# A hybrid diffusion step with expert retrieval: the latent phase entered before the prompt's routing, its products spread over the front, late chunks routed by pairs of heads

## The reference

```python
h = rmsnorm(x) * (1 + sc_a) + sh_a
q, k, v, xr, xg, ga, gr = split(h @ w_in)
attn = windowed attention(q, k, v)        # latent queries also read cached keys
rnn  = rglru(dwconv(xr))                  # forward and backward scan over the tokens
a_out = attn @ w_attn_o
r_out = (rnn * gelu(xg)) @ w_rnn_o
x = x + g_a * ((sigmoid(ga) * a_out + sigmoid(gr) * r_out) @ w_out)
h = rmsnorm(x) * (1 + sc_f) + sh_f
# experts, chunk by chunk of 128 tokens: 1 chunk of the prompt, 4 of the latent tokens
s = (h @ w_q) against 2 x 128 sub-keys for each of 8 heads
st, it = top_k(s, 16)                     # per head and side
best, pos = top_k(st[0][:, None] + st[1][None, :], 16)   # 16 experts of 16384 per head
e = it[0] * 128 + it[1] at pos
act = gelu(u_tab[e] . h)                  # 128 rows of 4 KB per token
x = x + g_f * sum(softmax(best) * act * v_tab[e])        # 128 more rows of 4 KB per token
y = rmsnorm(x)
```

## Time and profile before

| | us |
|---|---|
| median of 3 runs | 2618.7 |
| their range | 2607.69 to 2623.31 |
| the profiled execution | 2609.64 |
| its span in the trace | 2607.8 |
| DVE busy | 1808.8 (69%) |
| PE busy | 1918.0 (74%) |
| POOL busy | 1026.9 (39%) |
| ACT busy | 475.3 (18%) |
| DMA moved | 753.44 MB, mean 289 GB/s |

### The profile page before, as it was taken

One profiled execution on the slowest core, in us unless ns is written; L12 is line 12 of the kernel. 1 busy time (PEld: TensorE's weight loads), 2 busy tenths in 40 slices (PEclk: granted clock), 3 DMA queues, 4 the chain that ended last, 5 costly groups with the idle time before them and its releaser, 6 DMA issues.

```text
span 2607.8 us, 20641 instructions
## 1 busy us (share of the span) xinstructions
PE 1918.0 (74%) x6333; PEld 1129.0 (43%) x6333; DVE 1808.8 (69%) x3658; ACT 475.3 (18%) x1195; POOL 1026.9 (39%) x1028
## 2 busy tenths in 40 slices
PE   6789676989978999993666776469999999000085
PEld 2568552444437548441222333256666666000032
DVE  1341386987777115499888999788877566999955
ACT  0451201533004200111112342180000000000011
POOL 0000001324640000125776776634434445777574
PEclk9889787999989999997998998989999999555599
DMA  8656554657970032447999999959999999999997
GB/s 286 213 171 223 192 178 152 209 187 252 378 248 17 33 115 79 145 162 284 409 409 378 362 397 374 391 177 378 410 411 410 409 410 409 409 410 409 362 395 313
DMA packets 296873, 753.44 MB, mean 289 GB/s; under 512 B 21503, under 2 KB 141103, under 8 KB 296245
## 3 DMA queue, kind: packets, MB, share of 16 engines
q0 software_dynamic: 147456, 536.94, 53.6%
q1 hardware_dynamic: 149308, 215.20, 23.6%
HBM read 740.72 MB, written 11.33 MB: 288 GB/s over the span
## 4 chain that ended last, share of the span: by engine, by line
DVE 27%; DMA 25%; PE 22%; POOL 13%; issue 7%; ACT 4%; SPq 0%; ACTq 0%; DVEq 0%; POOLq 0%
DMA attn<-in_peer_u_dram,eidx 8%; PE pair L739 6%; PE bank L739 6%; DMA attn<-in_peer_v_dram,eidx 4%; DMA h_all<-in_peer_u_dram,eidx 4%; POOL attn L1918 4%; POOL big L1918 4%; DVE attn L1435 3%; DMA ring_more<-in_peer_u_dram,eidx 3%; ACT work L1032 3%; PE bank L913 3%; DMA big<-in_peer_u_dram,eidx 2%; POOL ring_more L1918 2%; POOL work L1918 2%; DVE big L1435 2%
## 5 line engine op out<-in xcount | busy, mean ns | idle before, releaser
L960 PE MATMUL bank<-big,work 128*128 128x512 f32 x380 | 205.8, 671 | 388.1 <-ACT work L1032 276.6
L1918 POOL DMA_INDIRECT attn<-in_peer_u_dram,eidx x200 | 198.0, 990 | 545.7 <-DVEq L1532 313.1
L739 PE MATMUL pair<-big 128*128 128x128 f32 (+1 forms) x1280 | 371.2, 449 | 26.7 <-DVEq L1327 17.9
L1918 POOL DMA_INDIRECT h_all<-in_peer_u_dram,eidx x106 | 121.2, 1143 | 586.3 <-DVEq L1798 420.5
L739 PE MATMUL bank<-big 128*128 128x512 f32 (+1 forms) x1056 | 314.2, 460 | 32.8 <-DVEq L1331 17.8
L960 PEld LDWEIGHTS bank<-big,work 128*128 128x128 f32 x380 | 71.6, 208 | 505.1 <-issue 433.8
L739 PEld LDWEIGHTS pair<-big 128*128 128x128 f32 x1280 | 202.7, 200 | 182.6 <-issue 169.2
L1435 DVE CUSTOM_DVE_ANT_0 attn<-attn,pair 128x1024 f32<-128x1024 f32 x200 | 240.9, 1219 | 54.3 <-DMA attn<-in_peer_u_dram,eidx 50.4
L1005 PE MATMUL bank<-h_all,big 128*128 128x512 f32 x608 | 269.0, 599 | 6.8 <-DMA h_all<-in_peer_v_dram 6.8
L739 PEld LDWEIGHTS bank<-big 128*128 128x128 f32 x1056 | 175.0, 208 | 167.2 <-issue 162.7
L1005 PEld LDWEIGHTS bank<-h_all,big 128*128 128x128 f32 x608 | 180.6, 297 | 91.1 <-DMA h_all<-in_peer_v_dram 8.2
(11 more groups left out here) (254 smaller groups left out, 2907.6 us busy)
## 6 DMA issues: line engine op xcount, KB each, us to landing
big<-in_w_in_dram SPq DMA_DIRECT2D x44, 1024.0 KB, 6.6
h_all<-in_peer_v_dram SPq DMA_DIRECT2D x76, 512.0 KB, 6.8
big<-in_peer_v_dram SPq DMA_DIRECT2D x52, 512.0 KB, 6.8
big<-in_w_ada_dram SPq DMA_DIRECT2D x24, 1024.0 KB, 7.6
big<-in_peer_w_q_dram SPq DMA_DIRECT2D x16, 1024.0 KB, 5.6
big<-in_w_rnn_o_dram SPq DMA_DIRECT2D x8, 1024.0 KB, 8.4
big<-in_w_attn_o_dram SPq DMA_DIRECT2D x8, 1024.0 KB, 5.0
big<-in_w_out_dram SPq DMA_DIRECT2D x8, 1024.0 KB, 7.9
```

The lines of the kernel that those rows point to most:

```text
L739: last = nc.tensor.matmul(u[:, 0:n], w[:, k, col:col + P], src[:, k, 0:n], start=(k == 0), stop=(k == KD - 1))
L960: last = nc.tensor.matmul(psum[i][:, :], diag[:, (n - 1) % DIAGS, :], ring[r][:, i * 512:(i + 1) * 512], start=(k == first_by_tensor[c]), ...
L1918: g.indirect_dma_start(dst, None, ins["peer_" + table][0], bass.IndirectOffsetOnAxis(ap=eidx[:, c, k:k + 1], axis=0)).then_inc(landed, 16)
```

## The change

It has three parts.

1. **Hand-over.** In the prompt's last stage ACT copies each score block to `scores0` in SBUF and frees its bank. PE, ACT and DVE have no `end_stage()` there. `load_lru()` (2 MB) moves from before the tile (1, "xr", 4) to before (1, "xr", 0). DVE does the prompt's `topk` in the latent recurrence, two in each block. The remaining routing of the prompt is 17 units, `route0`, that `serve` does before its products.
2. **Products spread.** `serve` does nothing inside the recurrence. After it: 6 units, 5 after each merge of `gr`, 1 after each rope, 2 and 1 in each attention quad, 4, 7 after each merge of `ga`, 2 after each `mix` unit. `gelu_dots(0)` moves into the `mix` stage, behind tile t = 1's units.
3. **Tail.** The prompt's v sets are 32 in step 0 and 96 in step 1 (three after four u). `route` is by pairs of heads: four `topk`, `best_of_64` (the 64 sums that can be among the best 16, in four blocks), `places_of_64`, two `expert_side`, `ids`. Of each late chunk two pairs are routed one step before the other two. The one-hots of step 1 are spread over the whole step, where they stood in its first two thirds. The ring has 29 buffers; in step 3's first 88 turns 9 are open (13 before), then 15 (13), at the end 19 (17). Step 3 starts with 64 u sets of C4 alone. v table tiles use other buffers, the first one loaded ahead instead of two.

```diff
-    half = SLOTS // 2
-    for k in range(SLOTS - EARLY):
-        n0, n1 = (j * half // (SLOTS - EARLY) for j in (k, k + 1))
-        steps[0] += [("u", C1, EARLY + k)] + [("v", 0, n) for n in range(n0, n1)]
-    for k in range(half):
-        steps[1] += [("u", C1 + 1, 2 * k), ("u", C1 + 1, 2 * k + 1), ("v", 0, half + k)]
+    V0_FIRST, V0_NEXT = 32, 96
+    for k in range(SLOTS - EARLY):
+        n0, n1 = (j * V0_FIRST // (SLOTS - EARLY) for j in (k, k + 1))
+        steps[0] += [("u", C1, EARLY + k)] + [("v", 0, 0 + n) for n in range(n0, n1)]
...
-    hots_at = [step_start[1] + len(steps[1]) * PH // PIECES * m // BUILDS for m in range(BUILDS)]
+    hots_at = [step_start[1] + len(steps[1]) * m // BUILDS for m in range(BUILDS)]
...
@@ block.sync @@
+                    if key == (1, "xr", 0):
+                        u = (0, "mix", D // TC - 1, NT[0] - 1)
+                        sp_.wait_ge(bank_full[bank[u]], use[u])
+                        load_lru()
                     if key == (1, "xr", 4):
-                        sp_.wait_ge(route_ready, CH0[ph])
-                        load_lru()
...
@@ block.scalar @@
                 def spread(hp):
                     u = full((ph, "sc", hp))
+                    if ph == 0:
+                        run(scores0[:, hp, :], u[:, 0:P], ACT.Identity).then_inc(bank_free[bank[(ph, "sc", hp)]], 1)
+                        return
...
-                end_stage()
-                if ph == 0:
-                    soft(0)
@@ block.vector @@
+            def route0(i):
+                if i < PH:
+                    best_sums(0, i)
+                elif i == PH:
+                    best_diffs(0)
+                elif i <= 2 * PH:
+                    experts(0, i - PH - 1, i - PH)
+                    ids(0, i - PH - 1, i - PH)
...
+            def best_of_64(c, h0):
+                tv = top_v[:, c - C1, 2 * h0:2 * h0 + 4, :].rearrange("p (h s) k -> p h s k", s=2)
+                a, b = tv[:, :, 0, :], tv[:, :, 1, :]
+                s2 = cand[:, 64 * h0:64 * (h0 + 2)].rearrange("p (h n) -> p h n", h=2)
+                for lo, i0, ni, nj in ((0, 0, 1, 16), (16, 1, 3, 8), (40, 4, 4, 4), (56, 8, 8, 1)):
+                    for h in range(2):
+                        mark(V.tensor_tensor(s2[:, h, lo:lo + ni * nj].rearrange("p (i j) -> p i j", i=ni),
+                                             a[:, h, i0:i0 + ni].unsqueeze(2).to_broadcast([P, ni, nj]),
+                                             b[:, h, 0:nj].unsqueeze(1).to_broadcast([P, ni, nj]), ALU.add))
...
+                for h in (h0, h0 + 1):
...
+                    link(V.max(v0, s))
+                    link(V.max_index(p0, v0, s))
+                    link(V.match_replace(s, v0, s, NEG_BIG))
+                    link(V.max(v1, s))
+                    link(V.max_index(p1, v1, s))
...
+            def route(c, pair, between):
+                for i in range(4):
+                    hp = 4 * pair + i
+                    topk(c - C1, hp, late2[:, hp, :] if c == C1 + 1 else late34[:, c - C1 - 2, hp, :])
+                    between(i)
+                h = 2 * pair
+                best_of_64(c, h)
+                between(4)
+                places_of_64(c, h)
+                expert_side(h, h + 2, 0)
+                between(5)
+                expert_side(h, h + 2, 1)
+                ids(c, h, h + 2)
...
-                    serve(2)
+                    for hp in (2 * j, 2 * j + 1) if ph else ():
+                        u = (0, "sc", hp)
+                        dve.wait_ge(bank_free[bank[u]], use[u])
+                        topk(-1, hp, scores0[:, hp, :])
...
-                        serve(8 if a == "gr" else 6)
-                serve(8)
+                        serve(5 if a == "gr" else 7)
+                serve(6)
...
-                    serve(4)
+                    serve(2)
...
-                    serve(2)
+                    serve(1)
                 end_stage()
-                serve(16)
+                serve(4)
                 merge("ga", "ao", KD)
...
-            pool.wait_ge(head_ready, PH)
             for n in range(SLOTS):
                 r = n % RING0
+                if n % TOPK == 0:
+                    pool.wait_ge(head_ready, n // TOPK + 1)
```

More of the change, by code:

```diff
@@ L429, in hybrid_step @@
         ring += [big[:, o_keys + i * D:o_keys + (i + 1) * D] for i in range(2)]
+        ring += [big[:, o_h + i * D:o_h + (i + 1) * D] for i in range(2)]
         assert len(ring) == RING
@@ L1187, in _ @@
                 for t in range(NT[ph] + 1):
+                    if ph and t == 1:
+                        gelu_dots(0)
                     if t < NT[ph]:
@@ L1886, in _ @@
                     add_prompt()
+            left = SLOTS - BUILDS // 2
+            for quarter, (c, pair) in enumerate(((C3, 2), (C3, 3), (C4, 0), (C4, 1))):
+                if quarter == 3:
+                    routed(C3)
+                n_rows = share(left, quarter, 4)
+                route(c, pair, lambda i: rows(share(n_rows, i, PARTS)))
             dve.wait_ge(final_in, 48)
             final(0, hot[:, 0:D])
[L1889 to L1892 removed]
             step_end(C3)
[L1895 removed]
+            for pair in (2, 3):
+                n_rows = SLOTS // 4
+                route(C4, pair, lambda i: rows(share(n_rows, i, PARTS)))
+            rows(SLOTS // 2)
+            routed(C4)
+            rows(step_start[4] - next_turn[0])
             step_end(C4)
```

198 lines of the change are left out of this document (106 added, 92 removed).

## The result

The changed kernel takes 2555.6 us (median of 4 runs, 2550.48 to 2557.03); the kernel before, run beside it, 2615.1 (2607.69 to 2623.31). The ratio is 0.977, its 95% interval 0.974 to 0.980. The forecast was 2556. The profiled execution took 2556.07 us with a span of 2554.3, where before it had 2609.64 and 2607.8.

What follows compares the result with a forecast made beforehand. Transfers bound the kernel from 1200 us on, mostly PE the latent front. Front -38 and behind it -19 gave 2609.6 - 57 = 2552.6 profiled, stated as a 2556 median; own range 2540 to 2575, whole range 2522 to 2602.

Steps and rivals of the forecast that it cites:

- Hand-over: Prompt's last stage to latent phase: PE no longer waits for DVE's routing, latent phase starts earlier; -45 us, bounds -35 and -46.
- Recurrence: Latent recurrence: products leave DVE's blocks, PE's 7.1 us wait goes and PE starts warm; -9.7 us, bounds 0 and -10.
- `gr`/`ro`/`q`: Stage after the recurrence: fewer products on DVE hold PE up, 144 us against 167.5; -23.5 us, bounds -15 and -26.
- Attention: Attention quads: 24 added products, partly fitting DVE's idle 22.1 us, lengthen the stage; +11.5 us.
- `ga`: `ga` merges: seven products each, hidden behind PE for the first four, DVE at 12.8 us each for the last; +16.5 us.
- `mix`: `mix` stage: 14 remaining products, 25.6 us, and `gelu_dots(0)` lengthen it to 78 us against 66.4; +12, bounds 0 and +20.
- Steps 0 and 1: Both steps become bound by transfers as v sets and routing move; -16 us, bounds 0 and -20.
- Steps 2 to 4: Added routing and step 3's opening with 9 buffers cost nothing, two more buffers at the end help; -3, bounds +3 and -6.
- The products give back more: Rival, chance 0.20: in attention, `ga` and `mix` each product delays its stage in full; 2588 us.
- Gathers land faster: Rival, chance 0.15: in attention and `ga` little else is moved, so products take 1.22 us; `ga` +5.6, `mix` +2, total 2532.
- PE's clock in step 1: Rival, chance 0.06: PE at the slower clock in three quarters of step 1's rounds, step 412 us, kernel 2668.
- The hand-over doesn't come: Rival, chance 0.04: at the latent phase's start, tiles or ACT hold PE as DVE did; 2588 us.

Runs made afterwards that it cites:

- run 1: The changed kernel with the 2 MB of recurrence weights issued after the first xr and xg tiles of the latent phase, not ahead of them: 2546.4 us.
- run 5: The changed kernel with no products in the first seven attention quads, more in the last quad, ahead of the first `ga` merge and in `mix`: 2552.0 us.
- run 4: The changed kernel with the prompt's v sets split 64 and 64 over steps 0 and 1 instead of 32 and 96: 2562.0 us, ratio 0.981.
- run 6: The changed kernel with the one-hots of step 1 in the first two thirds of the step again: 2577.2 us.
- runs 11 and 12: One kernel measured twice: run 10 with the four `experts` moved from the recurrence to behind it, `serve` counts adapted: 2605.2 and 2603.5 us, ratio 0.963 both.
- run 10: The changed kernel with weights later, seven buffers, products re-laid, more step 2 rows, `topk` at phase 0's end, `best_sums` and four `experts` in the recurrence: 2498.3 us.

## Why the prediction was right, term by term

The median was forecast at 2556 and came at 2555.6; the sum for the profiled execution, 2552.6, was 3.5 us too low. Both are closer than the terms deserve: in the front the tile (+4.9), `ga` (+6.8), `gr`/`ro`/`q` (+2.4) and attention (+1.2) came out dearer and `mix` (-9.6) cheaper. The mechanisms held but for `mix`, the cover in `ga` and a part of the recurrence; that the errors nearly cancel is luck.

**Hand-over, -45, measured -40.1.** PE's own part came out to the microsecond (372). Missed was the cover of the tile: "If they are late, a landing of 8 us and those 5 bring at most 10 us back" was the right mechanism, priced by bytes; run 1 shows 4.2 us. SP was 9.3 us at the four issues before it came to the tile, which a count of bytes doesn't tell.

**Recurrence, -9.7, measured -10.2.** Block 7's wait of 7.1 us is gone, as worked out; PE is busy 194.4 of 194.7. "PE also starts warm", 2.8 us of the sum, failed: PE again started after a wait, and the first 64 products took 29.4 us instead of 30.1. What came in its place was not in the sum: before, the 48 products right behind block 7's wait took 23.07 us at a granted clock of 0.90; without the wait they take 20.76 at 1.00. 7.1, 0.7 and 2.3 make 10.1.

**`gr`/`ro`/`q`, -23.5, measured -21.1.** PE's waits are 2.6 and 4.4, as forecast (2.5 and 4.4).

**Attention, +11.5, measured +12.7.** The size is right, and run 5 shows that it is the products' place in the quads. That a ring of 4 or 7 leaves it alone excludes the gathers.

**`ga`, +16.5, measured +23.3.** The step that failed is the cover and the pace: "For the first four merges PE needs 13.7 us each, the ring 7 x 1.83 = 12.8: hidden" and "For the last four PE needs 6.8 and DVE 12.8". Of the first rounds one took 16.4 us instead of 13.7, and the last four took 54.8, not 51.2. Seven products at 1.72 and 1.67 for the merge make 13.7. So a product was priced a little too high, and the merge beside the seven products left out. The upper bound, +20, was passed.

**`mix`, +12, measured +2.4.** The step that failed added 25.6 us of products to PE's units. Fourteen products were there as forecast, but beside PE: DVE is busy 51.4 of 68.8. Run 5 shows that seven more cost their full time.

**Front, -38, measured -33.0.** Two errors of opposite sign, +7 and -10, 5 from the tile, and 3 from the other terms.

**Steps 0 and 1, -16, measured -18.3.** Step 1 went to 404 GB/s, step 0 stayed at 406. The cause had been put to the moved v sets and the moved routing; run 4 gives 7 us to the split, and run 6 shows that the split needs the spread one-hots, which the forecast counted as "the same". How the other 11.3 us divide between spreading and routing by pairs is open. The 64-sum routing is as costed: `best_of_64` for two heads takes 3.85 us, between the first and the last row here,

```profile
1739.32 0.80 DVE L1534 TENSOR_TENSOR work<-big 128x16 f32<-128x16 f32 x8
...
1743.17 1.22 DVE L1467 CUSTOM_DVE_ANT_0 attn<-attn,pair 128x1024 f32<-128x1024 f32 x1
```

against 2 x 2.97; `places_of_64` takes 3.3 (1748.5 to 1751.9 us) where `expert_places` took 0.9: 0.3 more a pair, in the range 0 to 2.

**Steps 2 to 4, -3, measured -2.2.** That is about what this stretch varies by between runs with the same code; neither the larger ring nor the new opening of its buffers was tried alone.

**The rivals.** *The products give back more*: for `ga` it was right, for attention and `mix` not; 2588 didn't come. *Gathers land faster*: they did, 5.1 us in attention and 6.2 in `ga` where 7.9 had been read, but not by enough; a product in `ga` still took 1.72 us and not 1.22, and `ga` went the other way, +23.3. The Trainium skill (DMA: Bandwidth & Descriptors, "Anatomy of one DMA") gives an estimate of 3.2 us for such a gather. One that was alone in flight, issued at 815.65 us in attention's last quad, took 4.2, the nearest to it. *PE's clock in step 1*: a round is 299.5/32 = 9.4 us, just above the 9.3 that the prediction had named as a sign of being wrong, but not for the reason it feared: PE is busy 7.0 of it and granted 0.97, more than before. The granted clock rose with PE's work; in step 0, where PE lost work (125 products for 253), it fell to 0.71, and transfers stayed at 406 GB/s. *The hand-over doesn't come*: it came but for the tile.

**The signs.** PE's first 512-column product came at 377.3 instead of 370 to 375, `q`'s last unit ended at 713.9 instead of about 707, PE waited 24.9 us before `mix` instead of 17, and the queries came at 1011.2 instead of 1003 to 1010. The tile accounts for the first, for 5 of the second's 7 us and for the last; block 7, the quads (10.5 us each, by the gathers issued at 745.0 to 797.7 us, one quad's first to that of the fifth after it) and the transfers were as said.

## What to carry to other kernels

Filler work is free where its engine waits longest, not where its busy share is lowest: 27 products, most in the holes of attention's last quad and behind it, cost 0.9 us, 28 with three in each quad 12.7. Count the waits in the timeline one by one and cut the filler to fit them. When an engine leaves a stage, look at once at what is queued behind the transfers that the early start now needs. And where work is moved between two steps, move supply and consumer together: 32 more v sets in step 1 brought 7 us with its one-hots spread over the whole step, and lost all of the gain with the one-hots in the first two thirds.

## What was not expected of the hardware

- A gather's landing grew in `ga` with the number in flight, 5.8, 6.2 and 8.0 us at four, five and seven buffers, while the mean of the transfers rose from 298 to 333 and 390 GB/s; with five buffers it was 5.1 in attention, and 4.2 for one alone.
- Issuing 512 KB of recurrence weights held SP's queue 2.3 us (9.3 for four) each, right behind a 1 MB tile, and 1.7 in run 1 (6.7 for four); a 1 MB tile with nothing ahead held it 0.37 us, and the 1 MB tiles behind the weights 1.6 to 2.7. So what is still under way ahead counts; whether the weights' short rows count too isn't shown.
- DVE idle for a quarter of the recurrence was no room: 3.8 us of extra work a block cost nothing, 6.8 in six blocks 3.9 us, 7.1 in four 6.3, and in both it was one wait, 134 to 136 us into the stage, after which blocks ran on as before.
- In runs 11 and 12 transfers in steps 0 and 1 were slower with nearly the same kernel (339 and 360 GB/s in run 12, 406 and 402 in run 10), and the kernel before took 2707 and 2708 us beside them. No run here tells why.
